# Moving the first half's block inverse four places later in the slots of an RWKV-7 chain

## The reference, cut to what matters

```
s_kk = S kk_t
S    = S * w_t - s_kk (kk_t * a_t)^T + v_t k_t^T
y_t  = S r_t
```

## Time and profile before

| what | value |
|---|---|
| median of 3 runs | 3619.16 us (3611.99 to 3623.68) |
| the profiled execution | 3610.41 us, of it the span of the trace 3608.6 us |
| PE busy | 3447.1 us (96%) |
| DVE busy | 2487.9 us (69%) |
| ACT busy | 1156.4 us (32%) |
| POOL busy | 590.4 us (16%) |

### The profile page before, as it was taken

How to read it: one execution, slowest core, us unless ns; L and a number is a source line. 1 busy time by engine, 2 the same in 40 slices (tenths; PEclk the granted TensorE clock), 3 DMA queues, 4 the chain that set the end, 5 groups by cost and what they waited for, 6 DMA issues and landing times. The chain is left out here.

```text
span 3608.6 us, 74335 instructions
## 1 busy us (share of the span) xinstructions
PE 3447.1 (96%) x28653; PEld 2513.5 (70%) x28653; DVE 2487.9 (69%) x4562; ACT 1156.4 (32%) x2482; POOL 590.4 (16%) x1128
## 2 busy tenths in 40 slices
PE   7998998999999999999999999999999997888999
PEld 2447777688786455555888876678877456777887
DVE  7986665489897657653898954469987956664431
ACT  4035554133202444431233014323310225663210
POOL 1015553000000323320000000000000105553000
PEclk9998999999999999999999999999999998999999
DMA  6641111244353323223444520043434541111454
GB/s 219 207 136 24 21 22 32 74 133 130 118 161 97 105 79 102 82 76 99 129 126 127 162 83 28 25 126 121 136 118 129 170 129 25 25 24 27 134 152 133
DMA packets 584315, 365.07 MB, mean 101 GB/s; under 512 B 126144, under 2 KB 553480, under 8 KB 581928
## 3 DMA queue, kind: packets, MB, share of 16 engines
q1 hardware_dynamic: 557544, 250.40, 25.1%
q0 software_dynamic: 26432, 110.07, 8.7%
HBM read 348.73 MB, written 11.67 MB: 100 GB/s over the span
## 5 line engine op out<-in xcount | busy, mean ns | idle before, releaser
L275 PE MATMUL PS<-H,WR 128*128 128x512 f32 (+1 forms) x1424 | 477.1, 494 | 0.0
L591 DVE SCALAR_TENSOR_TENSOR WORK<-WORK,SC 128x512 f32<-128x512 f32 x616 | 418.3, 746 | 0.7
L275 PEld LDWEIGHTS PS<-H,WR 128*128 128x128 f32 x1424 | 268.0, 190 | 187.3 <-issue 167.2
L2549 PE MATMUL PS<-WORK 64*64 64x64 f32 (+2 forms) x6944 | 361.0, 231 | 29.5 <-ACT BIG L2846 16.6
L571 POOL DMA_DIRECT2D WORK<-in_ada_w_dram x88 | 66.4, 755 | 1857.7 <-DVE WORK L591 839.6
L1474 PE MATMUL PS<-BIG,WR 128*128 128x512 f32 (+1 forms) x944 | 329.4, 503 | 5.2 <-DMA WR<-in_rw_wo_dram 1.7
L2549 PEld LDWEIGHTS PS<-WORK 64*64 64x64 f32 (+1 forms) x6944 | 282.1, 139 | 69.2 <-ACT WORK L2835 23.0
L1474 PEld LDWEIGHTS PS<-BIG,WR 128*128 128x128 f32 x944 | 175.7, 190 | 132.6 <-issue 111.8
L2835 ACT ACTIVATE WORK<-PS 128x64 f32<-128x64 f32 (+3 forms) x528 | 161.4, 326 | 292.0 <-PE PS L2549 286.7
L1012 ACT ACTIVATE WORK<-PS 128x512 f32<-128x512 f32 x252 | 134.7, 541 | 335.6 <-PE PS L945 285.1
L945 PE MATMUL PS<-BIG 128*128 128x256 f32 x984 | 223.9, 380 | 0.0
(11 more groups left out here) (363 smaller groups left out, 6391.0 us busy)
## 6 DMA issues: line engine op xcount, KB each, us to landing
WORK<-in_ada_w_dram POOLq DMA_DIRECT2D x88, 1024.0 KB, 6.3
WR<-in_ffn_w_in_dram SPq DMA_DIRECT2D x220, 256.0 KB, 2.9
BIG<-in_ffn_w_in_dram SPq DMA_DIRECT2D x132, 256.0 KB, 3.4
WR<-in_ffn_w_out_dram SPq DMA_DIRECT2D x106, 256.0 KB, 2.8
WR<-in_ssd_w_in_dram SPq DMA_DIRECT2D x96, 256.0 KB, 2.8
BIG<-scratch_dram POOLq DMA_DIRECT2D x8, 2048.0 KB, 7.9
BIG<-in_ffn_w_out_dram SPq DMA_DIRECT2D x36, 256.0 KB, 3.2
BIG<-in_ada_w_dram SPq DMA_DIRECT2D x4, 2048.0 KB, 15.5
```

Of the source, the lines that this page charges most:

```text
L275: mm = pe.matmul(outs, WR[:, slot, k, 0:m], rhs(k), start=first and k == 0, stop=last and k == nk - 1)
L591: lag(vec.scalar_tensor_tensor(ACC3[:, s_], w, by, ACC3[:, s_], ALU.mult, ALU.add), label)
L2549: return pe.matmul(o, lhs, rhs, start=start, stop=stop)
```

## The change

In the even slots of tiles 1 to 7, in both layers, E moves from place 1 to place 5, and the eight joining steps move from places 4, 5, 7, 8, 10, 11, 13, 14 to places 8, 9, 11, 12, 14, 15, 17, 18. Tile 0 and all odd slots keep their places. Nothing is added or removed.

```
             if s == 0:
-                at = (4, 5, 7, 8, 10, 11, 13, 14) if i else (21, 21, 22, 22, 23, 23, 24, 24)
+                at = (8, 9, 11, 12, 14, 15, 17, 18) if i else (21, 21, 22, 22, 23, 23, 24, 24)
                 early += [(k, *step) for k, step in zip(at, levels)]
-                early += [(1 if i else 20, "E", i, 0), (0, "R", i, 0, 0), (2, "R", i, 0, 1), (9, "H2", both[0], 0),
+                early += [(5 if i else 20, "E", i, 0), (0, "R", i, 0, 0), (2, "R", i, 0, 1), (9, "H2", both[0], 0),
```

## The result

The changed kernel takes 3629.33 us (median of 11 runs, 3626.26 to 3637.48); the kernel before, run beside it on the same chip, 3620.16 us (3608.42 to 3623.68). The medians are 9.2 us apart; the ratio, which is worked out from all runs of both, is 1.0035 [1.0025, 1.0044] (the brackets hold its 95% interval), slower by about 12.6 us. The prediction (3632 us, slower by 0.36%) was right in sign, size and main mechanism; its POOL term was not, nor, in layer 0, one half of its rule for what the odd slots give back. The profiled execution took 3629.33 us with a span of 3627.5 us.

What follows compares the result with a forecast made beforehand. PE with the chain's latencies and the inverse's SP/POOL round trip bound the kernel by turns. 7.2 us (layer 0) + 6.0 us (layer 3) = 13 us on 3619.2 gives 3632 us, range 3615 to 3646 us.

Steps and rivals of the forecast that it cites:

- POOL term: The inverse's trip lengthens where E meets POOL's small instructions: 0.3 us a tile, bounds 0 and 0.84 us.
- Even slot of layer 0, +2.4 us: Even slots of layer 0: 2.0 us behind at place 7, restart 0.1, transpose wait 0.5, less 0.2; +2.4 us.
- The walk: Slot 6 of layer 0, stepped through with traced durations: second direction's W 0.57 us later, about 0.5 us transpose wait.
- Layer 3, +1.6 us: Even slots of layer 3: 1.4 us of joining products not yet done, later second-direction W; +1.6 us each.
- What the odd slots give back: Odd slots: E of the second half waits less when PE arrives later; more than half of 28 us taken back.
- the room: PE's wait in odd slots that can absorb lateness: 1.8 to 2.1 us, next to none in tiles 2 and 6 of layer 0.
- The rule for the give-back: Odd slot's end shift: larger of start shift less PE's wait and shift of the trip's start; 6.3 and 4.8 us at tile 7.
- The sum, 13 us: Whole kernel: 7.2 us for layer 0 plus 6.0 us for layer 3, giving 13 us slower.
- Faster: DVE not full at place 5, so first halves' landing waits (13 us) leave the path: 3606 us; chance 0.08.
- Absorbed: Second halves' landings stay, so only tiles 2 and 6 of layer 0 carry their even slot: 3624 us; chance 0.23.
- Much slower: Late second-direction S and late joins feed each other; even slots cost 3.5 us, less half: 3643 us; chance 0.07.
- What would show it: Even slots near 23.5 and 22.2 us, second-half E waits well under 30 us, PE waits over 1 us for L3205.

Runs made afterwards that it cites:

- the kernel with both edits: The changed kernel with E of the second halves at place 4 instead of 2: 3635.31 us, ratio 1.0046 to the kernel before.

## Why the prediction was right, step by step

- **Even slot of layer 0, +2.4 us.** Measured +2.5 (21.2 to 23.7 us in slots 6, 8, 10, 12). The walk held in the main: W of the second chunk kept its time in the slot (7.62 us behind its start before, 7.66 us now), since DVE's S cannot be earlier. The W of the second direction went from 9.55 to 10.35 us behind the start, 0.80 us in place of the 0.57 us forecast. The wait for the level's transpose was 0.31 us, not 0.5 us. The experiments split the growth into 1.27 us for the joins and, on top of them, 1.3 us for E.
- **Layer 3, +1.6 us.** Measured +1.8 in slots 4 and 10, +1.2 to +1.3 in slots 8 and 12, and 3.0 in slot 6, which has a stretch at the lower clock.
- **What the odd slots give back.** The forecast of shifts at the ends of the odd slots of layer 0, without the POOL term, was 0, 2.4, 2.7, 3.3, 3.9, 6.3, 6.3 us. Counted from the start of slot 0, the two profiles differ by -0.3, 2.2, 2.7, 3.4, 4.1, 6.6, 8.2 us. In this count slots 0 and 1, whose code is unchanged, took 1.9 us more, and slot 2, which waits for tile 1's inverse, took 2.1 us less. Slots 5 and 13 had no room and took 24.4 us as before (in the kernel with layer 3 changed, slot 5 did wait in unchanged code, and took 26.16 us); slots 7, 9 and 11 gave up their wait. Issuing KS three times shows that this is a property of the schedule and not of this edit, and the kernel with both edits that the room can be spent once only.
- **The rule for the give-back: one half of it failed in layer 0.** The rule takes the larger of two shifts: that at the slot's start less the room, and that of the trip's start one odd slot earlier. Followed to the letter it gives 4.8, 5.1, 7.5 and 7.5 us for tiles 4 to 7; the list has the first shift alone there, and the traces side with the list. The rule rests on SP having no gap between a tile's halves, which is so for tile 3 and for every tile of layer 3. Behind the first half of tile 4, however, SP stood for 2.0 us until ACT had copied the second half's GT (the kernel before):

```profile
448.26 0.37 SPq L2522 DMA_DIRECT2D WORK<-blocks_dram  x1
450.30 2.02 SPq L2499 DMA_DIRECT2D blocks_dram<-WORK  x2
```

For tiles 5 and 6 it was 2.0 and 2.4 us. These trips hang on the GT at places 19 and 20, behind the wait that the same slot gives back, and not on the first GT. So the landings of tiles 4, 5 and 6 moved by 3.7, 3.6 and 4.3 us where the first GT moved by 4.9, 5.3 and 6.1 us, and slots 7, 9 and 11, ahead of whose E DVE now waits 0.5 us at most, take 24.14 us. In layer 3 the rule's second half was used (0, 0.7, 1.6, 2.3, 3.2, 3.9, 4.8 us). The mean of three profiles with a changed layer 3 less that of two with the old one is 0.0, 1.2, 1.1, 3.9, 5.2, 6.0, 6.3 us, more than forecast; stretches at the lower clock and the slow round trip of slot 9 are in it.

- **The last slot of layer 0** varies in unchanged code, from 20.8 to 25.3 us, with the landing of tile 7's inverse. In the kernels with E at place 2, a landing 1.3 to 1.4 us into the slot goes with 20.8 us, one 2.9 us in with 22.3 us, and landings 2.6 to 3.4 us in that are followed by a stretch at the lower clock with 23.5 to 25.3 us.
- **The POOL term, 0.3 us a tile: this step failed.** The inverse of tile 3's second half ran on POOL from 410.28 to 423.43 us before and from 411.44 to 424.24 us now, 13.15 and 12.80 us. The same holds for tiles 2 to 7 in the mean: 12.3 and 12.1 us in two profiles with the old layer 0, 12.2, 12.1 and 12.0 us in three with the changed one; in layer 3 12.0 and 11.6 us against 11.5, 11.4 and 11.3 us. The whole trip of layer 0, from first GT to landing, got shorter (47.3 and 47.5 us against 46.5 to 46.7 us), not longer. E's two instructions now take 0.93 us together for 0.76 us, so DVE paid for the meeting, 0.09 us for each, and POOL's chain nothing in sum. By the rule of the Trainium skill (page "SBUF — State Buffer", section "Who interferes with whom") that I weighed, the term would have been at the upper bound, 0.84 us; the traces do not bear that price out here, though the dearer E agrees with the two getting in each other's way.
- **The sum, 13 us.** The ratio gives 12.6 us, the medians 9.2 us. That the sum came so close is in part luck: the POOL term (about 2 us) was not there, and costs that I had not thought of are. In slots 2 to 15 of both layers the clock was at the lower level for 13.7 us before, and for 17.1 and 20.5 us in two profiles of the change; at 1.2 to 1.5 us for each 3.4 us, that is an estimate of 1.2 to 3.0 us, from few profiles. The two profiles differ by more (18.9 us of span), because the profiled execution of the kernel before is a low one. Its layer 3, slots 2 to 15, takes 296.9 us, and the same unchanged code 302.7 us in the kernel with layer 0 changed; its layer 0 takes 325.1 us, against 327.3 us in the kernel with layer 3 changed. Three profiles with a changed layer 0 have 331.4, 332.2 and 330.6 us, three with a changed layer 3 306.7, 306.2 and 304.3 us. The means differ by 5.2 and 6.0 us, for the 7.2 and 6.0 us forecast; the two layers' ratios give 6.5 and 6.9 us.
- **The rivals.** Faster: its deciding point was DVE's S of the second direction staying where it was. It moved from 9.06 to 10.05 us behind the slot's start. Absorbed: its condition, that the landings of the second halves stay where they are, failed (they moved by 1.0 to 4.3 us), and tiles 3, 4 and 5 lost 0.5 to 0.7 us each as well, not only 2 and 6. Much slower: not here, but E one place later is that case (even slots +3.4 us in slot 10, 4.9 us in slot 6), through PE's wait at the Z and the clock.
- **What would show it.** Even slots near 23.5 and 22.2 us, odd ones at 24.1 to 24.4 and 20.6 to 22.3 us (but for the last slots, slot 3 of layer 0 and slot 9 of layer 3 with its slow round trip), the landing's wait at 17.3 us and at no first half, PE's wait of over 1 us for L3205: all there.

What stays open is why E at place 4 in the odd slots wins 0.2%. The medians show it. In the profiles the odd slots that waited win 0.3 to 0.8 us each and slots 2 and 15 of layer 0 about 3.4 us each, while slots 0, 1, 5 and 13 of layer 0 and 14 of layer 3 lose most of it again. The gain of slot 15 (23.91 to 20.53 us) is not E's place as such: the inverse landed 0.6 us into that slot in place of 3.2 us, half of it because slot 13 had become 1.2 us longer, and kernels with E at place 2 and a landing 1.3 to 1.4 us in took 20.8 us too. That E's new place takes away the dependence on a late landing in the other slots is argued, not shown.

## What to carry to other kernels

Filler work belongs where the chain makes its engine wait anyway. Before spreading it "more evenly", look for the places with a wait ahead of the chain's step in the timeline: a step taken out of such a hole costs most of its length (0.33 us for a Z of 0.47 us), and an instruction put ahead of a chain step on an engine that is full there costs the chain as well (1.3 us for an E of 1.6 us). When two resources bound a program by turns, price an edit by both: what one slot loses comes back in the next as long as that one waits for something, and the room is spent once. An edit that wins on one version of a schedule need not win on the next for that reason.

## What was not expected of the hardware

**The clock behind short waits.** The granted clock of PE has two levels in these traces, 1.00 (2.4 GHz) and 0.50 (1.2 GHz). Slot 6 of layer 3 after the change, in four windows (start, the stretch with PE's wait, the one behind it, the rest):

```profile
3120.22:3128.00 7.78, 5.55 (x81) 3.44 (x82) 5.07 (x10) 5.65 (x10) 0.43 (x2) 1.00 0.38 61
3128.00:3129.80 1.80, 0.75 (x4) 0.02 (x2) 1.62 (x5) 1.20 (x4) 1.35 (x6) 1.00 0.02 5
3129.80:3133.30 3.50, 3.50 (x66) 3.50 (x68) 0.92 (x2) 2.56 (x6) 2.85 (x9) 0.51 0.02 5
3133.30:3143.74 10.44, 10.15 (x332) 9.75 (x330) 6.68 (x21) 5.74 (x15) 5.61 (x15) 1.00 0.11 16
```

PE was idle for over 1 us of the 1.8 us ahead, then ran at a granted clock of 0.51 (1.2 GHz) without a gap for 3.50 us, and at 1.00 again. The slot took 23.52 us, its like without such a stretch 22.2 to 22.35 us: 1.2 to 1.3 us. Slot 10 of the same profile has the same waits ahead (0.72 and 1.17 us, here 0.72 and 1.05 us) and stayed at 1.00, so the waits alone do not decide. In slots 2 to 15 of the two layers the kernel before has three such stretches, two profiles of the change five each, mostly in other slots, and E one place later has one in eight of the 14 even slots. So a wait of PE can cost more than its length, and by a price that changes from run to run.

**A write and read back through DRAM** varies more than the one slot suggests. In the 384 half-trips of result out and back of all twelve profiles (layers 0 and 3, two per tile), the read was issued 1.9 us after the write in the median, but over 3 us after it in 39, and at most 3.8 us; from the read's issue to its landing it took 2.2 us in the median and over 3.5 us in 21. Slot 9 of layer 3 had both at once, 3.62 and 3.93 us, 7.55 us in all where the next longest is 6.40 us. It took 5.3 us more than in the second profile of the change (26.45 and 21.16 us). Little of that is left at the end of the layer: slots 2 to 15 took 306.7 us with it and 306.2 us without. The slots behind it took 3.7 us less than in that other profile, 1.1 us of it because slot 10 there had a stretch at the lower clock.
